# Expert blocks of 896 columns in a two-layer decoder trunk, with weights in 3.5 KB and 8 KB pieces

## What is computed

```python
D_FF_EXPERT = 7 * D_MODEL // 2          # 3584

def swiglu(x, w_gate, w_up, w_down):
    return (jax.nn.silu(x @ w_gate) * (x @ w_up)) @ w_down

def moe_swiglu(x, w_router, w_gate, w_up, w_down):
    logits = (x @ w_router).astype(jnp.float32)
    top_vals, top_idx = lax.top_k(logits, TOP_K)
    top_w = jax.nn.softmax(top_vals, axis=-1)
    gates = jnp.sum(jax.nn.one_hot(top_idx, N_EXPERTS, dtype=jnp.float32) * top_w[..., None], axis=-2)
    out = jnp.zeros_like(x)
    for e in range(N_EXPERTS):
        out = out + gates[..., e:e + 1].astype(x.dtype) * swiglu(x, w_gate[e], w_up[e], w_down[e])
    return out
```

## Time and profile before

| | |
|---|---|
| median of 3 runs | 1417.56 us (1417.31 to 1418.04) |
| profiled execution | 1417.98 us |
| its span, first to last instruction | 1416.2 us |
| mean granted TensorE clock | 0.992 |
| TensorE busy | 1347.7 us (95%) |
| VectorE busy | 1135.7 us (80%) |
| ScalarE busy | 980.9 us (69%) |
| HBM read, written | 437.99 MB, 15.75 MB |
| expert loads | 336 of 1024 KB |

### The profile page before, as it was taken

How to read it: one execution, slowest core, us unless ns; L and a number is a source line. 1 busy time by engine, 2 the same in 40 slices (tenths; PEclk the granted TensorE clock), 3 DMA queues, 4 the chain that set the end, 5 groups by cost and what they waited for, 6 DMA issues and landing times.

```text
span 1416.2 us, 19010 instructions
## 1 busy us (share of the span) xinstructions
PE 1347.7 (95%) x6759; PEld 1106.2 (78%) x6759; DVE 1135.7 (80%) x1013; ACT 980.9 (69%) x951; POOL 80.1 (6%) x112
## 2 busy tenths in 40 slices
PE   9999999999999899999999999999999998999987
PEld 8988888889997777777777777777777776777765
DVE  5776454467657798999999999999999998999986
ACT  6555443446547587788877778887778886777774
POOL 2000000000000680000000000000000002000000
PEclk9999999999999899999999999999999999999999
DMA  9758655586442899999999999999999999999980
GB/s 323 257 178 313 233 197 180 185 261 197 152 150 103 306 394 394 394 396 394 389 394 394 394 396 394 387 397 393 395 395 394 393 389 398 394 394 395 394 321 30
DMA packets 197726, 454.41 MB, mean 321 GB/s; under 512 B 7466, under 2 KB 28982, under 8 KB 197679
## 3 DMA queue, kind: packets, MB, share of 16 engines
q1 hardware_dynamic: 190944, 429.94, 82.2%
q0 software_dynamic: 4832, 17.13, 3.3%
q10 hardware_dynamic: 1902, 6.70, 1.4%
HBM read 437.99 MB, written 15.75 MB: 320 GB/s over the span
## 4 chain that ended last, share of the span: by engine, by line
DMA 42%; PE 33%; DVE 14%; ACT 9%; issue 2%; ACTq 0%; DVEq 0%; SPq 0%
DMA raw<-in_o_exp_up 40%; PE bank L1122 15%; DVE w_lo L1829 11%; ACT w_hi L623 8%; PE bank L1156 5%; PE bank L1430 4%; PE bank L1317 1%; DMA raw<-in_o_ple_gate 1%; PE bank L1222 1%; PE bank L1701 1%; PE bank L1242 0%; PE bank L1732 0%; DMA h<-in_x 0%; PE bank L1630 0%; PE bank L1272 0%
## 5 line engine op out<-in xcount | busy, mean ns | idle before, releaser
L1829 DVE TENSOR_TENSOR w_lo<-raw,w_hi 128x2048 fp32r<-128x2048 f32 x406 | 926.8, 2290 | 210.0 <-ACT w_hi L623 205.8
L623 ACT ACTIVATE w_hi<-raw 128x2048 fp32r<-128x2048 f32 x406 | 777.6, 1919 | 299.7 <-PE bank L1122 79.3
L1688 PE MATMUL bank<-w_lo,x_hi 128*128 128x512 f32 x448 | 132.5, 417 | 43.0 <-DVE w_lo L1829 41.9
L1688 PEld LDWEIGHTS bank<-w_lo,x_hi 128*128 128x128 f32 x448 | 77.2, 189 | 92.7 <-DVE w_lo L1829 80.9
L1685 PE MATMUL bank<-w_hi,x_hi 128*128 128x512 f32 x448 | 124.4, 399 | 1.9 <-ACT w_hi L623 1.9
L1669 PE MATMUL bank<-w_hi,x_hi 128*128 128x512 f32 x448 | 123.1, 397 | 0.1
L1676 PE MATMUL bank<-w_lo,x_hi 128*128 128x512 f32 x448 | 120.3, 390 | 0.7 <-DVE w_lo L1829 0.5
L1673 PE MATMUL bank<-w_hi,x_lo 128*128 128x512 f32 x448 | 120.1, 390 | 0.0
L1122 PE MATMUL bank<-w_hi,x_lo 128*128 128x512 f32 (+1 forms) x304 | 108.5, 357 | 0.3 <-DVE x_lo L1863 0.3
L1122 PE MATMUL bank<-w_lo,x_hi 128*128 128x512 f32 (+1 forms) x304 | 108.1, 356 | 0.0
L1122 PE MATMUL bank<-w_hi,x_hi 128*128 128x512 f32 (+1 forms) x304 | 108.1, 356 | 0.0
(11 more groups left out here) (331 smaller groups left out, 1829.3 us busy)
## 6 DMA issues: line engine op xcount, KB each, us to landing
raw<-in_o_exp_gate SPq DMA_DIRECT2D x112, 1024.0 KB, 11.5
raw<-in_o_exp_up SPq DMA_DIRECT2D x112, 1024.0 KB, 11.6
raw<-in_o_exp_down SPq DMA_DIRECT2D x112, 1024.0 KB, 11.4
raw<-in_o_w_qkv SPq DMA_DIRECT2D x12, 1024.0 KB, 5.3
raw<-in_e_ffn_gate SPq DMA_DIRECT2D x11, 1024.0 KB, 5.1
raw<-in_e_ffn_up SPq DMA_DIRECT2D x11, 1024.0 KB, 5.4
raw<-in_e_ffn_down SPq DMA_DIRECT2D x11, 1024.0 KB, 4.8
raw<-in_e_w_in SPq DMA_DIRECT2D x9, 1024.0 KB, 14.2
```

Of the source, the lines that this page charges most:

```text
L623: act.activation(w_hi[:, slot % SPLIT], raw[:, slot], ACT.Copy).then_inc(hi_made, 1)
L1688: mm = pe.matmul(dst, x_two[:, c + kk, :], lo[:, kk], start=False, stop=(c, kk) == (4, 3))
L1829: ve.tensor_tensor(w_lo[:, slot % SPLIT], raw[:, slot], w_hi[:, slot % SPLIT], ALU.subtract).then_inc(lo_made, 1)
```

## The change

Blocks of 896 columns (`CUT`, seven chunks of 128) take the place of steps of 512: four blocks for seven steps. A block has 24 tiles instead of 12. Gate and up tiles hold two chunks of rows with 896 columns (1792 elements per partition, 896 KB, pieces of 3.5 KB). Down tiles hold 256 rows such that two neighbouring rows lie in one partition (pieces of 8 KB); the last down tile of a block has 128 rows and 512 KB. A result of 896 columns stands in two banks, 448 in each, and PSUM is allocated as four pairs of banks. Gate uses pair 0, up uses pair 1, and the turned hidden values and the folded small results use pair 1 as well; the small down sum is in pair 2 and the wide one in pair 3. Since a partition of a down tile holds rows 2p and 2p + 1, the transposes and the fold take every other column (`chunk_of`). The tiles of a block come in a new order, which alternates between the experts. G and U are wide gate and up, g and u small, D and d down; small down tiles belong to the block before:

The fold stands after the second tile and the turn after the twelfth. ScalarE, VectorE and SyncE follow this order; silu is written over `hid`. In the opening `gather_small` stands between up tiles. Between jobs both halves of `turn_rows` stand together, and at the end `y_wide` stands before the splits of the embedding's tiles. The core of the diff:

```diff
-BLOCKS = D_FFE // HALF
+CUT = 7 * P
+BLOCKS = D_FFE // CUT
+PARTS = CUT // P
+UP = 2 * CUT
...
-STEP_TILES = 12
+STEP_TILES = 24
+SKIP = 4
...
+        banks = [ctx.enter_context(nc.psum_tensor(f"banks{i}", [P, 2 * HALF], F32)) for i in range(4)]
+        bank = [banks[i // 2][:, i % 2 * HALF:(i % 2 + 1) * HALF] for i in range(8)]
+        gate_out, up_out = [in_halves(banks[i][:, :])[:, :, 0:CUT // 2] for i in range(2)]
+        turned = banks[1][:, 0:CUT]
+        gate_fold, up_fold = banks[1][:, 0:PARTS * SMALL], banks[1][:, HALF:HALF + PARTS * SMALL]
...
+        def chunk_of(q):
+            first = q // 2 * 2 * P
+            return slice(first + q % 2, first + 2 * P, 2) if q < PARTS - 1 else slice(first, first + P)
...
+            eg = o_exp_gate[0].rearrange("e (c p) (b n) -> e b p c n", p=P, n=CUT)
+            eu = o_exp_up[0].rearrange("e (c p) (b n) -> e b p c n", p=P, n=CUT)
+            by_block = o_exp_down[0].rearrange("e (b r) n -> e b r n", r=CUT)
+            ed = by_block[:, :, 0:(PARTS - 1) * P].rearrange("e b (i p c) n -> e b i p c n", p=P, c=2)
+            ed_last = by_block[:, :, (PARTS - 1) * P:].rearrange("e b (c p) n -> e b p c n", p=P)
+
+            def up(w, e, of, k, i, j, b):
+                load(tile_at(i, j, b), w[e, of, :, 2 * k:2 * k + 2], slot=(MOE_T - SKIP + i) % RAW)
+
+            def down(e, of, k, i, j, b):
+                load(tile_at(i, j, b), ed[e, of, k] if k < 3 else ed_last[e, of], slot=(MOE_T - SKIP + i) % RAW)
...
+            def wide_up(first, k, i, j, b, rows=None):
+                hi, lo = up_tiles(i)
+                def product(x, w, start=False, stop=False):
+                    for kk in range(2):
+                        for f in range(2):
+                            mm = pe.matmul(bank[first + f][:, 0:CUT // 2], x[:, 2 * k + kk, 0:P], w[:, kk, f * (CUT // 2):(f + 1) * (CUT // 2)],
+                                           start=start and kk == 0, stop=stop and kk == 1, skip_group_check=True)
+                    return mm
+                wait_high(tile_at(i, j, b))
+                product(x_hi, hi, start=k == 0)
+                product(x_lo, hi)
+                wait_tile(tile_at(i, j, b))
+                product(x_hi, lo, stop=k == 3).then_inc(tile_used, 1)
...
+            def second_half(j, b, turn_next=False, first=False, placing=False, stop=False):
+                wide_down(0, 16, j, b, start=first or b is None)
+                small_up(2, 0, 17, j, b)
+                wide_down(1, 18, j, b)
+                small_up(2, 1, 19, j, b)
+                if turn_next:
+                    pe.wait_ge(s_copied, 2 * step_no(j, b) - 1)
+                    turn_rows(j + 1)
...
+                wide_down(2, 20, j, b)
+                small_up(2, 2, 21, j, b)
+                wide_down(3, 22, j, b, stop=stop)
+                small_up(2, 3, 23, j, b)
+
+            def step(b, j, start=False, turn_next=False, first=False, placing=False, stop=False):
+                pe.wait_ge(s_copied, 2 * step_no(j, b, 0) - 1)
+                wide_up(0, 0, 0, j, b)
+                wide_up(0, 1, 1, j, b)
+                fold_small(j, b)
+                wide_up(0, 2, 2, j, b)
+                wide_up(0, 3, 3, j, b)
+                pe.wait_ge(s_hid_made, step_no(j, b, 0))
+                wide_up(2, 0, 4, j, b)
+                small_down(0, 5, j, b, start=start)
+                wide_up(2, 1, 6, j, b)
+                small_down(1, 7, j, b)
+                wide_up(2, 2, 8, j, b)
+                wide_up(2, 3, 9, j, b)
+                pe.wait_ge(e_silu_made, step_no(j, b))
+                small_up(0, 0, 10, j, b)
+                small_up(0, 1, 11, j, b)
+                turn_wide(j, b)
+                small_down(2, 12, j, b)
+                small_up(0, 2, 13, j, b)
+                small_down(3, 14, j, b, stop=first)
+                small_up(0, 3, 15, j, b)
+                second_half(j, b, turn_next, first, placing, stop)
```

More of the change, by code:

```diff
@@ new lines, in _, with second_half @@
+            ed_last = by_block[:, :, (PARTS - 1) * P:].rearrange("e b (c p) n -> e b p c n", p=P)
[3 more added lines that the diff above has]
+                load(tile_at(i, j, b), ed[e, of, k] if k < 3 else ed_last[e, of], slot=(MOE_T - SKIP + i) % RAW)
+            def second_half(wide, small, of, j, b):
+                for k in range(4):
+                    down(wide, of, k, 16 + 2 * k, j, b)
+                    up(eu, small, of, k, 17 + 2 * k, j, b)
@@ new lines, in superstep @@
+            def superstep(wide, of, small_was, of_was, small, j, b):
+                for k in range(4):
+                    up(eg, wide, of, k, k, j, b)
+                up(eu, wide, of, 0, 4, j, b)
+                down(small_was, of_was, 0, 5, j, b)
+                up(eu, wide, of, 1, 6, j, b)
+                down(small_was, of_was, 1, 7, j, b)
+                up(eu, wide, of, 2, 8, j, b)
+                up(eu, wide, of, 3, 9, j, b)
+                up(eg, small, of, 0, 10, j, b)
+                up(eg, small, of, 1, 11, j, b)
+                down(small_was, of_was, 2, 12, j, b)
+                up(eg, small, of, 2, 13, j, b)
+                down(small_was, of_was, 3, 14, j, b)
+                up(eg, small, of, 3, 15, j, b)
+                second_half(wide, small, of, j, b)
@@ L622, in split @@
                 act.wait_ge(tile_loaded[slot], 16 * rounds + 16)
-                act.activation(w_hi[:, slot % SPLIT], raw[:, slot], ACT.Copy).then_inc(hi_made, 1)
+                act.activation(w_hi[:, slot % SPLIT, 0:size], raw[:, slot, 0:size], ACT.Copy).then_inc(hi_made, 1)
             def load_table(use, function):
@@ L1823, in link, with split @@
                 ve.wait_ge(vec_step, steps[0])
-            def split(n, slot=None):
+            def split(n, slot=None, size=TILE):
                 slot = n % RAW if slot is None else slot % RAW
                 ve.wait_ge(hi_made, n + 1)
-                ve.tensor_tensor(w_lo[:, slot % SPLIT], raw[:, slot], w_hi[:, slot % SPLIT], ALU.subtract).then_inc(lo_made, 1)
+                ve.tensor_tensor(w_lo[:, slot % SPLIT, 0:size], raw[:, slot, 0:size], w_hi[:, slot % SPLIT, 0:size], ALU.subtract)\
+                    .then_inc(lo_made, 1)
             def rsqrt(i):
```

522 lines of the change are left out of this document (261 added, 261 removed).

## The result

The changed kernel took 1446.57 us, the median of four runs (1445.54 to 1455.74), beside 1417.48 us (1417.31 to 1418.04) for the kernel before on the same chip: a ratio of 1.0217, 95% interval 1.0181 to 1.0252. The prediction was 1386 us, range 1378 to 1410: wrong in its sign and outside its range.

A forecast was written before the change was run, and what follows sets the result against it. The expert stage was taken as bound by transfer, with TensorE and VectorE just beneath. From 1417.98 us, 28 for the stage, 2 for the opening and 2 for the end were taken off: 1386 us, range 1378 to 1410.

The forecast's parts named there:

- Transfer rates: Expert stage: larger pieces move faster, 407 GB/s for gate and up at 3.5 KB, 423 for down at 8 KB.
- transfer's 53.4 us a block: Expert stage: gate and up 36.1 us plus down 17.4 us of transfer a block, against 55.8 for 1.75 old steps.
- case B: Rival for gate and up transfers: rate follows layout, not piece size; 1409 us, or 1400 with half the gain; chance 0.09.
- the term of 38 us: Expert stage: transfer time saved over 16 blocks by larger pieces, at 53.4 us a block for 55.8.
- case C: Rival for fold and turn: reading every other column as weights is slow; at twice the time 1448 us; chance 0.10.
- An ordinary block: Expert stage: 54.2 us a block with stalls and handovers, 1.6 less than before; computing bounds 52.4 to 55.4.
- The order: Tile order within a block: how evenly transfer, TensorE and VectorE share it; about 1 us of stalls, 54.2 us a block.
- Both turn_rows halves stand together: Turning the next rows: 2.2 us more from VectorE and ScalarE in three blocks, while transfer has 7 us of other work.
- The traffic of the job changes: Job changes: 21 us of other transfers delay transfer, not computing, so the stage gain is taken as 28 us, not 26.
- The opening: Start of the expert stage: moving the small gather between up tiles gains between 0 and 6 us, taken as 2.
- The end: After the last expert bytes: last fold, down tiles and scatter, between +5 and -5 us, taken as -2.
- case A: Rival in the expert stage: VectorE's late-block load falls whole on TensorE, 55.0 to 55.4 us a block, 1401 to 1410; chance 0.20.

The follow-up runs named there:

- e9: e5 with TensorE leaving out the products of high weights with low rows in the wide expert's gate and up; transfers, splits and copies kept: 1394.09 us.
- e5: e2's straight code, and the next job's rows turned three tiles earlier in a job's third block: 1405.82 us, 0.9926 of the kernel before.
- e1: The changed kernel run again without any edit, as yardstick for the others: 1445.75 us.
- e2: The changed kernel with TensorE's loop over the first three jobs written out as straight code, so no jump back: 1419.03 us, 1.0022 of the kernel before.
- e10: The changed kernel with its loop over the jobs kept and only the earlier turning of the next rows: 1436.87 us.
- e4: The kernel before with only TensorE's inner loop over the middle blocks written out, a body of 1986 instructions: 1425.22 us, ratio 1.0056.

## Why the prediction was wrong, step by step

- **Transfer rates: right; transfer's 53.4 us a block: too low.** Forecast 407 GB/s for gate and up, measured 405. For 8 KB 423, measured 418 in a stretch where 327 of 488 full packets are that long and the rest shorter. The size sets the rate, not the spread rows (case B falls). But the term of 38 us took these rates for the whole block. With TensorE relieved (e9) a block takes 54.4 us, so that even there transfer gives no more than 16 x (55.9 - 54.4) = 24 us.
- **VectorE's and TensorE's operations: right.** 1792 elements took 2021 ns, 1024 took 1216 and 896 took 1082, as forecast:

```profile
L1919 DVE TENSOR_TENSOR w_lo<-raw,w_hi 128x1792 fp32r<-128x1792 f32 x247 | 496.3, 2021 | 70.7 <-ACT w_hi L667 68.8
...
L1919 DVE TENSOR_TENSOR w_lo<-raw,w_hi 128x1024 fp32r<-128x1024 f32 x31 | 37.7, 1216 | 0.0
L2375 DVE TENSOR_TENSOR m_lo<-banks,m_hi 128x896 fp32r<-128x896 f32 x16 | 17.3, 1082 | 0.0
```

- **Spaced weights (case C): free.** 14 loads of the fold in 1.79 us are 0.128 each, 16 unspaced ones in the earlier trace rows 0.124; the turn's are 0.134 for 0.145. The measured time lies beside the 1448 of case C by chance: its mechanism is not there.
- **An ordinary block: nearly right.** 54.8 for 54.2 (54.7 as straight code), inside the bounds of 52.4 to 55.4, against 55.8. The "about 1 us of stalls" is there: in e5 TensorE waits 15.2 us for low splits from 560 to 1340 us, 1.1 a block.
- **The failed step: 54.2 us for every block of the stage.** "The order" weighed waits between tiles, and the code the engine must execute was no term at all. I read that the inner loop had gone and did not ask what length that gave the outer one. Two jumps back cost 26.7 us (e1 to e2). Each is 5.4 and 3.6 us of gap and about 4 us lost to the half clock by the records, so some 13.
- **"Both turn_rows halves stand together and take 2.2 us more from VectorE and ScalarE in three blocks; transfer has 7 us of other work there": failed.** The delay was laid on two engines with something else to do, and what was late next, TensorE's first tile of block 4, was not followed. Moving it gained 13.2 us in straight code (e2 to e5; 8.8 of it seen at the job changes) and 8.9 with the loop.
- **"The traffic of the job changes ... gives computing some time back": failed.** Even in e5 the two blocks around each change take 56.1 to 56.9 and 57.3 us. Against 15 ordinary intervals of 54.7, e5 has 18.6 us too many from first to last fold (1351.05 - 511.97 = 839.1); the kernel before, against 27 of 31.93, has 14.9 (1365.88 - 488.84 = 877.0). All that goes beyond ordinary blocks there, the seams, costs 3.7 us more where I took 2 less. The job change brings turning, sums and copies, which are computing; when computing sets the pace, they are paid. But by the folds the three job changes come to 12.8 us in e5 and 11.2 before, so that more than half of the 3.7 lies elsewhere, in the first block and in the last job (its block with the placing takes 58.8 us).
- **The opening** (2 us gained forecast): e5's first fold comes at 512.0 us, for 488.8 plus three quarters of a step, 512.8: 0.8 us gained. The first fold stands two tiles into its block where it stood one tile into its step, and the last one has no such tile before it, so an estimate in equal work shifts 1.9 us (2 x 54.7 / 24 less 31.9 / 12): 2.7 gained at the opening, as forecast, and 5.6 lost at the seams. **The end** (2 gained forecast): from the last fold on, 51.9 us in e5, 55.1 in e2 and 56.7 in the changed kernel, for 50.3: a loss, inside its bound of 5 but for the changed kernel's first profile.

The sum: 1446.6 less 26.7 (jumps) less 13.2 (turning) is 1406.7. That it meets the 1405.8 of e5 proves nothing, since both terms are differences on the way to e5; what tests them is e10, where the turning alone gives 8.9. The profiled span of e5 is 1402.9 us where the forecast's would be 1384.2 (1386 less the 1.8 between time and span), 18.7 more. Of these, ordinary blocks are 8.3 (26 forecast, and 15 x (55.88 - 54.7) = 17.7 between the first and the last fold), the seams 5.7 (3.7 and the 2 credited), the opening 1.2 and the end 3.5, together 18.7. A version without the two faults has the time of case A (computing takes over, 1401 to 1410), but only in part its mechanism: its ordinary blocks take 54.7 us, under the 55.0 to 55.4 of that case, and the rest was lost at the seams and the end. None of my cases was about code.

## What to carry to other kernels

When an edit writes out steps inside a loop, or gives steps different bodies, count the instructions of the loop body for each engine. On TensorE a body of 1630 or more cost 5 us and more at each jump back, and 13 us each where computing had no slack; straight code had no such gap. When a bound by transfer is lowered to within 1 or 2% of computing, every wait that transfer used to cover comes to light at its full price, with the half clock behind it, so follow each moved step to TensorE's next matmul. And put the cost of a regular block and the cost of the seams between jobs in separate terms: here the first was right within 1%, and the seams decided.

## What the runs showed of the hardware

- The gap behind a jump back depended hardly at all on how far the body exceeded the limit (5.38 us at 1630 instructions, 5.40 at 2151), and has a second part (3.5 to 4.5 us) shortly behind it with the changed kernel's code. A second block is fetched just before that part ends (in the stretch 748 to 749 us; the gap ends at 750.61). The old order showed only the first part clearly (e4: one gap of 5.25).
- 68 products over 32 columns took 9.41 us, 0.138 each, against 0.20 for 448 columns, and in the records the clock fell behind them to its lower level although TensorE was never idle: 0.79 as the mean while they ran and 0.68 in the 4.8 us behind them.

```profile
551.00:560.20 9.20, 9.20 (x68) 9.20 (x68) 5.52 (x3) 3.48 (x2) 0.00 (x0) 0.79 1.04 400
560.20:565.00 4.80, 4.80 (x20) 3.92 (x19) 0.00 (x0) 0.24 (x1) 0.00 (x0) 0.68 1.05 386
```
